# Cross attention of a two-block network: the order of its four units, where softmax reads from, and where its outputs go

## The chip, the cores and the metric

The kernel runs on one core of a Trainium2 chip. TensorE (PE in the profile) does matmuls and transposes, VectorE (DVE) and ScalarE (ACT) do elementwise work, SyncE (SP) and GpSimd (POOL) start transfers. PE writes to PSUM, eight banks of 128 partitions x 512 float32; everything else lives in SBUF. The metric is the device time of one execution in microseconds, as a median of several.

## The reference

Two blocks of layers on a sequence of 256 tokens, width 2048. The change touches only the cross attention of the second block: 256 queries against 256 memory rows, 4 heads of 128.

```python
def memory_cross_attention(hn, mem_n, w_q, w_kv, w_o):
    ...
    q = (hn @ w_q).reshape(B, S, CROSS_HEADS, CROSS_HEAD)
    k, v = split_cols_2(mem_n @ w_kv, (CROSS_HEADS * CROSS_HEAD, CROSS_HEADS * CROSS_HEAD))
    ...
    s = jnp.einsum('bshd,bmhd->bhsm', q, k).astype(jnp.float32) * (CROSS_HEAD ** -0.5)
    prob = jax.nn.softmax(s, axis=-1).astype(v.dtype)
    o = jnp.einsum('bhsm,bmhd->bshd', prob, v).reshape(B, S, CROSS_HEADS * CROSS_HEAD)
    return o @ w_o
```

Before it stands `h = h + mix(...)`, behind it the up and down products of the feed-forward part.

## The kernel before

Every engine has one instruction stream of its own, written by hand, and semaphores between them. Most of the time goes into large products that are done as `stream`s of **chunks**. A chunk is 512 rows of a weight matrix by 512 columns (1 MB). SP loads it into one of four buffers `weights_raw`; ACT copies it, rounded to float32r, into one of two buffers `weights_hi` (L671, function `hi`); DVE writes the rest, raw minus hi, into `weights_lo` (L1257, function `lo`); PE does 24 matmuls of 512 columns with it (L2054): the high part of the activations times both parts, and their low part times the high one. The activations of a product are therefore needed as two tiles, `acts_hi` and `acts_lo`. ACT may split chunk c when PE is through with chunk c-2 of the whole program (`chunk_used`), DVE follows ACT (`hi_ready`), PE follows DVE (`lo_ready`), and SP may load over a raw buffer once DVE has read it.

Four PSUM banks (0 to 3) hold the sums of the streams. The other four are a ring for everything else: each **job** in the list `job_counts` takes the next one, so a job waits until the job four places before it was read (`bank_free`), its reader waits until it is written (`bank_full`), and whoever needs the copy waits for the reader (`copied`).

The stage in question: `stream(cross_kv)` makes keys and values, `stream(cross_q)` (one block, four chunks) the queries; both come out through ACT (L687) in natural layout. PE transposes keys (`ckT`) and queries (`cqT`), two jobs each of four 128x128 transposes (L2125), ACT copies them (L951). Then come four **units** u, each a pair of heads and a half of the queries. For each unit PE computes scores (L2375, one bank of 2x256), DVE scales and copies them to SBUF (L1662), takes their row maximum (L1668) and negates it (L1669); ACT takes the exponentials in place with their row sums (L1028); DVE inverts the sums (L1675) and multiplies (L1677); PE transposes the probabilities (L2385, one bank of 4x128), ACT copies them (L1016); PE multiplies them with the values (L2396) and ACT copies the result to `acts_T` (L1022). PE's order is scores(0), scores(1), probs(0), outputs(0), scores(2), probs(1), outputs(1), scores(3), and so on; the probabilities have two buffers. When all four results are in `acts_T`, ACT and DVE split them (L786, L1327) for `stream(cross_o)`, a product with four blocks of one chunk each, whose first chunk they split only then. DVE adds each block to the residual (L2005).

Names that the text uses: `hi(0)`, `lo(0)` are the splits of the first chunk of `cross_o`; `hi(1)`, `lo(1)` those of the second.

Of the kernel before, what the change touches and what calls it, by code (L numbers as in the profile page):

```python
# [7 lines left out]
F32 = mybir.dt.float32  # L8
F32R = mybir.dt.float32r
I32 = mybir.dt.int32  # L10
ALU = mybir.AluOpType
# [4 lines left out]
P = 128  # L16
# [118 lines left out]
def build(nc, a, out, stop=None):  # L135
# [129 lines left out]
    CSP = place("cross_probs", 195.5, [P, 2, 2, T])  # L265
    CPT = place("cross_probs_T", 199.5, [P, 2, NB])
# [100 lines left out]
    def attention_jobs(pre, units):  # L367
        out_ = []
        for u in range(units + 1):
            if u < units:  # L370
                out_.append((f"{pre}_s{u}", 1))
            if u >= 1:
                out_ += [(f"{pre}_p{u - 1}", 1), (f"{pre}_o{u - 1}", 1)]
        return out_

# [12 lines left out]
    job_counts += attention_jobs("cross", 4)  # L388
# [77 lines left out]
    ACTS = {"ctx": 0, "lat": 4, "mix": 8, "cross_o": 12}  # L466
# [195 lines left out]
    def _(eng):  # L662
# [346 lines left out]
        def attention_steps(pre, SPb, PTb, dst, f0):  # L1009

            def probs_copy(u):
                jj = J[f"{pre}_p{u}"]
                if u >= 2:
                    bank_full(eng, J[f"{pre}_o{u - 2}"])
                bank_full(eng, jj)
                free(eng.activation(PTb[:, u % 2, :], bank(jj), ACT.Copy), jj)  # L1016

            def out_copy(u):
                pair, half = u // 2, u % 2
                jj = J[f"{pre}_o{u}"]  # L1020
                bank_full(eng, jj)
                free(eng.activation(dst[:, f0 + 2 * pair:f0 + 2 * pair + 2, half * P:(half + 1) * P],  # L1022
                                    bank(jj)[:, 0:T].rearrange("p (a b) -> p a b", a=2), ACT.Copy), jj)

            def exps(u):
                eng.wait_ge(S(pre + "_shifted"), u + 1)
                for e in range(2):
                    ch.add(eng.activation(SPb[:, u % 2, e, :], SPb[:, u % 2, e, :], ACT.Exp,  # L1028
                                          bias=STAT[:, 64 + 4 * (u % 2) + e:65 + 4 * (u % 2) + e],
                                          accum_out=STAT[:, 66 + 4 * (u % 2) + e:67 + 4 * (u % 2) + e]))  # L1030
                ch.done(pre + "_exp")

            return exps, probs_copy, out_copy

        def softmax_rows(pre, units, SPb, PTb, dst, f0):
            exps, probs_copy, out_copy = attention_steps(pre, SPb, PTb, dst, f0)
            for u in range(units):
                exps(u)
                if u >= 1:
                    probs_copy(u - 1)  # L1040
                    out_copy(u - 1)
            probs_copy(units - 1)
            out_copy(units - 1)

# [206 lines left out]
    def _(eng):  # L1251
# [399 lines left out]
        def attention_steps(pre, SPb, scale, bias):  # L1651

            def shift(u):
                half = u % 2
                m = 64 + 4 * (u % 2)
                if u >= 2:
                    bank_full(eng, J[f"{pre}_p{u - 2}"])
                jj = J[f"{pre}_s{u}"]
                bank_full(eng, jj)
                sc = bank(jj).rearrange("p (a b) -> p a b", a=2)  # L1660
                if bias is None:
# [21 lines left out]
        def softmax_rows(pre, units, SPb, scale, bias):  # L1683
            shift, divide = attention_steps(pre, SPb, scale, bias)
            for u in range(units):
                shift(u)
                divide(u)
# [1121 lines left out]
```

## Time and profile before

| | |
|---|---|
| median of 3 runs | 2879.57 us (2877.43 to 2879.62) |
| the profiled execution | 2869.85 us, span 2868.0 us |
| PE busy | 2574.4 us, 90% of the span |
| DVE, ACT busy | 1373.8 us (48%), 1102.1 us (38%) |
| chain that ended last | PE 59%, DVE 9%, ACT 4% |
| granted TensorE clock, mean | 0.922 of 2.4 GHz |

The span runs from the first to the last instruction that the profile shows. All times in rows are microseconds from its start. PE's matmul rows overlap each other, so its busy time is larger than its share of the chain. The granted clock is 1.00 at 2.4 GHz and 0.50 at 1.2 GHz; values between are means over a stretch in which both occurred.

### The profile page before, as it was taken

The page shows a single profiled execution, that of the slowest core. Times are in us where ns is not written, and L with a number is a line of the kernel's source. Part 1 is how long each engine was busy: PE and PEld are TensorE (multiplying, and loading weights), DVE is VectorE, ACT ScalarE, POOL GpSimd, SP SyncE. Part 2 cuts the span into 40 slices and gives each one's busy share as a digit, 9 for nine tenths or more (in the row PEclk, how much of TensorE's full clock was granted, in tenths as well). Part 3 has the DMA queues.
Part 4 walks back from the last instruction along what each step waited for, and adds up shares of the span by engine and source line. Part 5 has one row for each costly group of instructions (what it writes and reads, how often), then busy time and mean ns, then how long its engine had stood idle before and what let it go on. Part 6 is the DMA issues. An engine that isn't in the chain of part 4 may idle for free.

```text
span 2868.0 us, 30832 instructions
## 1 busy us (share of the span) xinstructions
PE 2574.4 (90%) x12600; PEld 2040.4 (71%) x12600; DVE 1373.8 (48%) x1331; ACT 1102.1 (38%) x1105; POOL 44.0 (2%) x77
## 2 busy tenths in 40 slices
PE   5799999999798999797999776889779999999996
PEld 0486787886477677576888655677668888888885
DVE  0234434557736533457444585444345544544543
ACT  1434435343333333434433343234444433434332
POOL 0000000001000000000000000000000000000000
PEclk8798989999998999798999677889889999999998
DMA  9843434558954774454554000254235555555553
GB/s 392 305 150 132 147 123 145 176 191 344 386 190 149 249 257 168 153 186 134 185 185 141 1 7 23 72 190 161 88 117 177 191 191 191 188 190 186 186 197 109
DMA packets 227546, 498.68 MB, mean 174 GB/s; under 512 B 25144, under 2 KB 27192, under 8 KB 218080
## 3 DMA queue, kind: packets, MB, share of 16 engines
q1 hardware_dynamic: 220752, 459.44, 46.8%
q0 software_dynamic: 6672, 37.51, 3.5%
q8 instruction: 90, 1.47, 0.2%
q14 instruction: 32, 0.26, 0.0%
HBM read 493.24 MB, written 3.67 MB: 173 GB/s over the span
## 4 chain that ended last, share of the span: by engine, by line
PE 59%; DVE 9%; ACT 4%; DMA 1%; issue 1%; DVEq 0%; POOL 0%; ACTq 0%
PE banks L2054 52%; DVE weights_lo L1257 1%; DMA raw_eight<-in_w_ada 1%; ACT weights_hi L671 1%; PE banks L2125 1%; ACT acts_hi L752 1%; PE banks L2512 1%; DVE index_scores L1756 1%; PE banks L2339 1%; DVE shifted_tile L1318 1%; PE banks L2260 1%; PE banks L2297 1%; PE banks L2355 0%; PE banks L2580 0%; PE banks L2243 0%
## 5 line engine op out<-in xcount | busy, mean ns | idle before, releaser
L1257 DVE TENSOR_TENSOR weights_lo<-weights_raw,weights_hi 128x2048 fp32r<-128x2048 f32 (+3 forms) x368 | 815.6, 2219 | 1042.4 <-ACT weights_hi L671 1041.5
L671 ACT ACTIVATE weights_hi<-weights_raw 128x2048 fp32r<-128x2048 f32 (+3 forms) x368 | 682.4, 1858 | 1142.0 <-PE banks L2054 1138.6
L2054 PE MATMUL banks<-weights_hi,acts_hi 128*128 128x512 f32 (+3 forms) x2432 | 967.5, 398 | 92.6 <-DVE weights_lo L1257 81.7
L2054 PE MATMUL banks<-weights_lo,acts_hi 128*128 128x512 f32 (+3 forms) x2432 | 956.0, 393 | 0.0
L2054 PE MATMUL banks<-weights_hi,acts_lo 128*128 128x512 f32 (+3 forms) x2432 | 955.4, 393 | 0.0
L2054 PEld LDWEIGHTS banks<-weights_hi,acts_hi 128*128 128x128 f32 x2432 | 476.0, 196 | 212.0 <-issue 76.3
L2054 PEld LDWEIGHTS banks<-weights_hi,acts_lo 128*128 128x128 f32 x2432 | 475.7, 196 | 94.7
L2054 PEld LDWEIGHTS banks<-weights_lo,acts_hi 128*128 128x128 f32 x2432 | 476.9, 196 | 92.1 <-issue 1.0
L2054 PE MATMUL banks<-weights_hi,hidden_hi 128*128 128x512 f32 x256 | 99.9, 390 | 0.0
L2054 PE MATMUL banks<-weights_hi,hidden_hi_odd 128*128 128x512 f32 x256 | 99.8, 390 | 0.0
L2054 PE MATMUL banks<-weights_hi,hidden_lo 128*128 128x512 f32 x256 | 99.7, 389 | 0.0
L2054 PE MATMUL banks<-weights_hi,hidden_lo_odd 128*128 128x512 f32 x256 | 99.7, 389 | 0.0
L2054 PE MATMUL banks<-weights_lo,hidden_hi 128*128 128x512 f32 x256 | 99.7, 389 | 0.0
L2054 PE MATMUL banks<-weights_lo,hidden_hi_odd 128*128 128x512 f32 x256 | 99.7, 389 | 0.0
L2147 PE MATMUL banks<-raw_eight,cond 128*2 128x512 f32 x256 | 54.6, 946 | 46.6 <-DMA raw_eight<-in_w_ada 36.6
L2147 PEld LDWEIGHTS banks<-raw_eight,cond 128*2 128x2 f32 x256 | 3.6, 83 | 94.0 <-DMA raw_eight<-in_w_ada 83.1
L2054 PEld LDWEIGHTS banks<-weights_hi,hidden_lo 128*128 128x128 f32 x256 | 48.1, 188 | 10.1
L2054 PEld LDWEIGHTS banks<-weights_hi,hidden_hi_odd 128*128 128x128 f32 x256 | 48.1, 188 | 10.0
L2054 PEld LDWEIGHTS banks<-weights_hi,hidden_lo_odd 128*128 128x128 f32 x256 | 48.1, 188 | 10.0
L2054 PEld LDWEIGHTS banks<-weights_lo,hidden_hi_odd 128*128 128x128 f32 x256 | 48.1, 188 | 9.9
L2054 PEld LDWEIGHTS banks<-weights_lo,hidden_hi 128*128 128x128 f32 x256 | 48.1, 188 | 9.9
L2054 PEld LDWEIGHTS banks<-weights_hi,hidden_hi 128*128 128x128 f32 x256 | 48.1, 188 | 9.9
(481 smaller groups left out, 1943.0 us busy)
## 6 DMA issues: line engine op xcount, KB each, us to landing
raw_eight<-in_w_ada SPq DMA_DIRECT2D x80, 1024.0 KB, 17.0
weights_raw<-in_w_in_e SPq DMA_DIRECT2D x80, 1024.0 KB, 5.3
weights_raw<-in_w_up SPq DMA_DIRECT2D x64, 1024.0 KB, 5.4
weights_raw<-in_w_down SPq DMA_DIRECT2D x64, 1024.0 KB, 5.0
weights_raw<-in_w_in SPq DMA_DIRECT2D x44, 1024.0 KB, 5.1
weights_raw<-in_w_in_o SPq DMA_DIRECT2D x32, 1024.0 KB, 5.3
weights_raw<-in_w_out_e SPq DMA_DIRECT2D x16, 1024.0 KB, 5.5
gate_chunks<-in_w_ada POOLq DMA_DIRECT2D x16, 1024.0 KB, 5.8
```

The lines of the kernel that those rows point to most:

```text
L671: eng.activation(WHI[:, c % 2, :, 0:n], RAW[:, sl, :, 0:n], ACT.Copy).then_inc(hi_ready, 1)
L752: ins = eng.activation(xh[:, f0 + f, :], bank(jj)[:, e * T:(e + 1) * T], func or ACT.Identity, scale=scale(f), bias=bias(f) if bias else 0.0)
L1257: eng.tensor_tensor(WLO[:, c % 2, :, 0:n], RAW[:, c % 4, :, 0:n], WHI[:, c % 2, :, 0:n].bitcast(F32), ALU.subtract).then_inc(lo_ready, 1)
L1318: ch.link(eng.tensor_scalar(TILE[:, e, :], src, scale(f), bias(f), ALU.mult, ALU.add))
L1756: ch.link(eng.scalar_tensor_tensor(out=SC[:, half, :], in0=RL[:, j % 2, e, :], scalar=KIWI[:, half, 64 + hd:65 + hd], in1=SC[:, half, :], ...
L2054: ins = eng.matmul(BANKS[:, par * 2 + h, 0:s.n], x[:, t, h * P:(h + 1) * P], w[:, c % 2, k, 0:s.n], start=(kc == 0 and k == 0 and m == 0), ...
L2125: ins = eng.transpose(bank(jj)[:, (f % 2) * T + h * P:(f % 2) * T + (h + 1) * P], src(f, h), ident)
L2147: ins = eng.matmul(BANKS[32 * j:32 * j + 2, 2 * hf, :], CF[:, kt, :], RAW8[:, m % 8, j, :], start=(kt == 0), stop=(kt == KT - 1))
L2260: ins = eng.matmul(bank(jj)[:, o0:o0 + P], A[:, 2 * hd + k2, h * P:(h + 1) * P], B[:, 2 * hd + k2, h * P:(h + 1) * P], start=(k2 == 0), st ...
L2297: ins = eng.matmul(dst, DECAYED[16 + d][:, 2 * hd + k2, B * P:(B + 1) * P], S0[:, d, hd, k2, :], start=False, stop=(d == 1 and k2 == 1))
L2339: ins = eng.matmul(bank(jj)[32 * j:32 * j + 2, :], CF[:, m, :], GCH[:, m % 2, j, :], start=(m == 0), stop=(m == KT - 1))
L2512: ins = eng.matmul(bank(jj)[:, q * P:(q + 1) * P], A[r, f, half * P:(half + 1) * P], B[r, f, half * P:(half + 1) * P], start=True, stop=True)
```

## The change

Six edits, all in this stage:

1. The transposes of the keys move from behind `stream(cross_q)` to behind its second chunk on PE, and their copies on ACT from behind it to the place after the sum of squares that follows its last split.
2. All four scores come first on PE, each in a ring bank of its own; then probs(0), probs(1), probs(2), outputs(0), probs(3), outputs(1), outputs(2), outputs(3). The ring's order follows. `cross_probs` gets four buffers, `cross_probs_T` keeps two.
3. DVE's scaled copy is gone. The maximum is read from PSUM, the exponential too, with the scale inside the activation.
4. The statistics have a place for each unit, so no unit waits for another's.
5. `acts_T` is left out: ACT copies each unit's output from PSUM to `acts_hi`, DVE subtracts that from PSUM into `acts_lo`.
6. The attention steps of ACT and DVE now stand inside `stream(cross_o)`, behind the split of its first chunk: `hi(0)` and `lo(0)` come before the first exponential and the first maximum.

```diff
+    job_counts += [(f"cross_s{u}", 1) for u in range(4)]
+    job_counts += [(f"cross_{n}", 1) for n in ("p0", "p1", "p2", "o0", "p3", "o1", "o2", "o3")]
...
-        stream(st["cross_q"], after={3: lambda: rms_squares(XN, 4, Y)})
-        tiles_out("ckT", CKT)
+        stream(st["cross_q"], after={3: lambda: (rms_squares(XN, 4, Y), tiles_out("ckT", CKT))})
         tiles_out("cqT", CQT)
-        softmax_rows("cross", 4, CSP, CPT, XS, 0)
-        wait_jobs("cross_o3")
-        split_hi(XS, 0)
-        stream(st["cross_o"])
+
+        def cross_exp(u):
+            eng.wait_ge(S("cross_max"), u + 1)
+            jj = J[f"cross_s{u}"]
+            for e in range(2):
+                ins = eng.activation(CSP[:, u, e, :], bank(jj)[:, e * T:(e + 1) * T], ACT.Exp, scale=128.0 ** -0.5,
+                                     bias=STAT[:, 64 + 4 * u + e:65 + 4 * u + e],
+                                     accum_out=STAT[:, 66 + 4 * u + e:67 + 4 * u + e])
+                if e == 0:
+                    ch.add(ins)
+            free(ins, jj)
+            copied(eng, jj)
+            ch.done("cross_exp")
+
+        def cross_probs_copy(u):
+            if u >= 2:
+                bank_full(eng, J[f"cross_o{u - 2}"])
...
+        def cross_hi(u):
+            jj = J[f"cross_o{u}"]
+            bank_full(eng, jj)
+            ch.add(eng.activation(cross_tiles(XTH, u), bank(jj)[:, 0:T].rearrange("p (a b) -> p a b", a=2), ACT.Copy))
+            ch.done("cross_hi")
+
+        def cross_attention():
+            for step, u in ((cross_exp, 0), (cross_exp, 1), (cross_exp, 2), (cross_probs_copy, 0), (cross_exp, 3),
+                            (cross_probs_copy, 1), (cross_probs_copy, 2), (cross_hi, 0), (cross_probs_copy, 3),
+                            (cross_hi, 1), (cross_hi, 2), (cross_hi, 3)):
+                step(u)
+
+        stream(st["cross_o"], after={0: cross_attention})
...
-        softmax_rows("cross", 4, CSP, 128.0 ** -0.5, None)
-        split_lo(XS, (0,), ACTS["cross_o"])
-        stream(st["cross_o"], sum_block(st["cross_o"], "h_block"))
+
+        def cross_max(u):
+            m = 64 + 4 * u
+            jj = J[f"cross_s{u}"]
+            bank_full(eng, jj)
+            ch.link(eng.tensor_reduce(STAT[:, m:m + 2], bank(jj).rearrange("p (a b) -> p a b", a=2), AX.X, ALU.max))
+            ch.add(eng.tensor_scalar(STAT[:, m:m + 2], STAT[:, m:m + 2], -(128.0 ** -0.5), None, ALU.mult))
+            ch.done("cross_max")
...
+        def cross_lo(u):
+            pair, half = u // 2, u % 2
+            jj = J[f"cross_o{u}"]
+            eng.wait_ge(S("cross_hi"), u + 1)
+            bank_full(eng, jj)
+            xl, xh = [t[:, 2 * pair:2 * pair + 2, half * P:(half + 1) * P] for t in (XTL, XTH)]
+            free(eng.tensor_tensor(xl, bank(jj)[:, 0:T].rearrange("p (a b) -> p a b", a=2), xh.bitcast(F32),
+                                   ALU.subtract), jj)
+
+        def cross_attention():
+            for step, u in ((cross_max, 0), (cross_max, 1), (cross_divide, 0), (cross_max, 2), (cross_divide, 1),
+                            (cross_max, 3), (cross_divide, 2), (cross_divide, 3), (cross_lo, 0), (cross_lo, 1),
+                            (cross_lo, 2), (cross_lo, 3)):
+                step(u)
+
+        stream(st["cross_o"], sum_block(st["cross_o"], "h_block"), after={0: cross_attention})
...
+        def cross_keys():
+            eng.wait_ge(block_out, 4 + 2 * st["cross_q"].b0)
+            transposes("ckT", natural(CKV))
+
+        stream(st["cross_q"], after={1: cross_keys})
         eng.wait_ge(block_out, 4 + 2 * st["cross_o"].b0)
-        transposes("ckT", natural(CKV))
         transposes("cqT", natural(CQ))
         jobs_out(eng, "cqT")
-        attention("cross", 4, CQT, CKT, lambda hd: hd, lambda g, sh: CKV[:, 1, sh, g * P:(g + 1) * P], CSP, CPT)
...
+        for u in range(4):
+            cross_scores(u)
+        for step, u in ((cross_probs, 0), (cross_probs, 1), (cross_probs, 2), (cross_outputs, 0), (cross_probs, 3),
+                        (cross_outputs, 1), (cross_outputs, 2), (cross_outputs, 3)):
+            step(u)
         stream(st["cross_o"])
```

What stands on PE from the first scores on, before. The rows with `cross_k_T` are scores, those with `constants` are transposes of the probabilities, those with `cross_probs_T` are outputs; a `side_free` is the release of a ring bank.

```order
L2375 MATMUL banks<-cross_k_T,cross_q_T 128x256 [waits side_free3,side_free2,side_free1,side_free0]
L2375 MATMUL banks<-cross_k_T,cross_q_T 128x256
L2375 MATMUL banks<-cross_k_T,cross_q_T 128x256 [waits side_free3]
L2375 MATMUL banks<-cross_k_T,cross_q_T 128x256
L2385 MATMUL banks<-constants,cross_probs 128x128 [waits side_free0,cross_probs]
L2385 MATMUL banks<-constants,cross_probs 128x128 x3
L2396 MATMUL banks<-cross_probs_T,cross_kv 128x128 [waits side_free1,side_free0]
L2396 MATMUL banks<-cross_probs_T,cross_kv 128x128 x3
L2375 MATMUL banks<-cross_k_T,cross_q_T 128x256 [waits side_free2]
L2375 MATMUL banks<-cross_k_T,cross_q_T 128x256
```

The same place on PE in the changed kernel, from the third unit's scores on.

```order
L2699 MATMUL banks<-cross_k_T,cross_q_T 128x256 [waits side_free0]
L2699 MATMUL banks<-cross_k_T,cross_q_T 128x256
L2699 MATMUL banks<-cross_k_T,cross_q_T 128x256 [waits side_free1]
L2699 MATMUL banks<-cross_k_T,cross_q_T 128x256
L2709 MATMUL banks<-constants,cross_probs 128x128 [waits side_free2,cross_probs]
L2709 MATMUL banks<-constants,cross_probs 128x128 x3
L2709 MATMUL banks<-constants,cross_probs 128x128 [waits side_free3,cross_probs]
L2709 MATMUL banks<-constants,cross_probs 128x128 x3
L2709 MATMUL banks<-constants,cross_probs 128x128 [waits side_free0,cross_probs]
L2709 MATMUL banks<-constants,cross_probs 128x128 x3
L2720 MATMUL banks<-cross_probs_T,cross_kv 128x128 [waits side_free1,side_free2]
L2720 MATMUL banks<-cross_probs_T,cross_kv 128x128 x3
```

Scores of units 2 and 3 no longer stand behind the outputs of units 0 and 1, and three transposes stand ahead of the first output.

DVE in the changed kernel, from the last step before the attention on (L1326 belongs to `stream(cross_q)`).

```order
L1326 RECIPROCAL inverse_rms<-inverse_rms 128x2 [waits dve_steps,root_out]
L1246 TENSOR_TENSOR weights_lo<-weights_raw,weights_hi 128x2048 [waits dve_steps,hi_ready]
L1974 TENSOR_REDUCE stats<-banks 128x2 [waits side_full2]
L1975 TENSOR_SCALAR stats<-stats 128x2 [waits dve_steps]
L1974 TENSOR_REDUCE stats<-banks 128x2 [waits dve_steps,side_full3]
L1975 TENSOR_SCALAR stats<-stats 128x2 [waits dve_steps]
L1981 RECIPROCAL stats<-stats 128x2 [waits dve_steps,cross_exp]
L1983 TENSOR_SCALAR cross_probs<-cross_probs,stats 128x256 [waits dve_steps]
L1983 TENSOR_SCALAR cross_probs<-cross_probs,stats 128x256
L1974 TENSOR_REDUCE stats<-banks 128x2 [waits dve_steps,side_full0]
```

The first row that reads scores (L1974) stands behind a whole `weights_lo` of 2048 columns, which before came after the attention.

ACT in the changed kernel, from the copies of the queries on.

```order
L943 ACTIVATE cross_q_T<-banks 128x512 [waits side_full0]
L943 ACTIVATE cross_q_T<-banks 128x512 [waits side_full1]
L663 ACTIVATE weights_hi<-weights_raw 128x2048 [waits chunk_used,chunk_landed0]
L1194 ACT_TABLE_LOAD
L1194 ACTIVATE cross_probs,stats<-banks,stats 128x256 [waits cross_max]
L1194 ACTIVATE cross_probs,stats<-banks,stats 128x256
```

`weights_hi` of the first chunk moved from behind the attention to the place before the table load and the first exponential.

## Rows read from the trace of the kernel before

**Rows 1.** The chain that ended last, 2040 to 2115 us: start, length, what.

```profile
2056.42 1.27 ACT cross_q L687 x2
...
2061.74 0.70 DVE cross_probs L1662
...
2063.44 1.10 ACT cross_probs L1028 x4
...
2088.03 0.39 ACT acts_T L1022
...
2088.50 1.06 ACT acts_hi L786
...
2089.73 1.92 ACT weights_hi L671
...
2091.67 2.30 DVE weights_lo L1257
...
2094.11 20.96 PE banks L2054 x83
```

**Rows 2.** Timeline of PE: start, length, group, idle time before it and what ended it.

```profile
2057.74 1.09 PE L2125 MATMUL banks<-constants,cross_kv 128*128 128x128 f32 x8 [1.42 <-ACT cross_q L687]
2058.67 1.04 PE L2125 MATMUL banks<-constants,cross_q 128*128 128x128 f32 x8
2060.60 1.97 PE L2375 MATMUL banks<-cross_k_T,cross_q_T 128*128 128x256 f32 x8 [0.89 <-ACT cross_q_T L951]
2065.54 0.66 PE L2385 MATMUL banks<-constants,cross_probs 128*128 128x128 f32 x4 [2.98 <-DVEq L451]
2069.14 2.07 PE L2396 MATMUL banks<-cross_probs_T,cross_kv 128*128 128x128 f32 x8 [2.95 <-ACT cross_probs_T L1016]
...
2072.72 1.06 PE L2385 MATMUL banks<-constants,cross_probs 128*128 128x128 f32 x4
2076.61 1.21 PE L2396 MATMUL banks<-cross_probs_T,cross_kv 128*128 128x128 f32 x8 [2.83 <-ACT cross_probs_T L1016]
```

**Rows 3.** Timeline of ACT, same columns.

```profile
2060.51 1.28 ACT L1028 ACT_TABLE_LOAD   x1
...
2068.50 0.60 ACT L1016 ACTIVATE cross_probs_T<-banks 128x512 f32<-128x512 f32 x1
...
2101.79 1.92 ACT L671 ACTIVATE weights_hi<-weights_raw 128x2048 fp32r<-128x2048 f32 x1 [8.35 <-PE banks L2054]
2107.23 1.92 ACT L671 ACTIVATE weights_hi<-weights_raw 128x2048 fp32r<-128x2048 f32 x1 [3.52 <-PE banks L2054]
```

**Rows 4.** Timeline of DVE, same columns.

```profile
2063.18 0.17 DVE L1669 TENSOR_SCALAR stats<-stats 128x2 f32<-128x2 f32 x1
2064.61 0.17 DVE L1675 RECIPROCAL stats<-stats 128x2 f32<-128x2 f32 x1 [1.26 <-ACTq L451]
2064.81 0.62 DVE L1677 TENSOR_SCALAR cross_probs<-cross_probs,stats 128x256 f32<-128x256 f32 x2
```

**Rows 5.** Groups by line and shape: busy us, mean ns, idle before.

```profile
L1886 DVE TENSOR_REDUCE stats<-banks 128x2 f32<-128x512 f32 x4 | 2.8, 692 | 11.7 <-PE banks L2557 11.6
...
L1886 DVE TENSOR_REDUCE stats<-banks 128x2 f32<-128x256 f32 x4 | 1.7, 424 | 7.1 <-PE banks L2557 7.1
...
L1135 ACT ACTIVATE probs<-banks,stats 128x256 f32<-128x256 f32 x8 | 3.7, 469 | 19.7 <-DVEq L451 19.7
```

**Rows 6.** Windows from start to end: length, busy PE, PEld, DVE, ACT, POOL, granted clock, DMA.

```profile
2066.00:2074.00 8.00, 4.83 (x18) 3.77 (x16) 2.83 (x8) 2.07 (x6) 0.00 (x0) 0.58 0.00 0
2074.00:2078.00 4.00, 1.39 (x9) 1.35 (x10) 1.40 (x5) 1.83 (x6) 0.00 (x0) 0.93 0.00 0
...
2085.00:2098.00 13.00, 6.14 (x18) 4.92 (x18) 5.72 (x3) 5.75 (x5) 0.00 (x0) 0.50 0.21 64
2098.00:2104.00 6.00, 6.00 (x27) 4.88 (x26) 1.55 (x3) 1.92 (x1) 0.00 (x0) 0.99 0.60 213
```

**Rows 7.** DMA issues of SP: start, length, op, count.

```profile
2032.08 18.09 SPq L499 DMA_DIRECT2D weights_raw<-in_w_o_cross  x4
```

More of the change, by code:

```diff
@@ L463, in acc @@
         return BANKS[:, (B % 2) * 2 + h, :]
[L466 removed]
+    ACTS = {"ctx": 0, "lat": 4, "mix": 8}
     def mlp_streams(stream, tile_step, at, first=None):
@@ L1007, in _ @@
         rms_squares.n = 0
[L1009 to L1043, printed above, removed]
         eng.wait_ge(S("norm_cols"), 2)
@@ L2744, in _, with cross_scores, cross_probs, cross_outputs @@
         transposes("x3T", natural(XN), ("h_block", 0))
-        stream(st["cross_q"])
+        def cross_keys():
+            eng.wait_ge(block_out, 4 + 2 * st["cross_q"].b0)
+            transposes("ckT", natural(CKV))
+        stream(st["cross_q"], after={1: cross_keys})
         eng.wait_ge(block_out, 4 + 2 * st["cross_o"].b0)
-        transposes("ckT", natural(CKV))
         transposes("cqT", natural(CQ))
         jobs_out(eng, "cqT")
-        attention("cross", 4, CQT, CKT, lambda hd: hd, lambda g, sh: CKV[:, 1, sh, g * P:(g + 1) * P], CSP, CPT)
+        def cross_scores(u):
+            pair, half = u // 2, u % 2
+            jj = J[f"cross_s{u}"]
+            bank_free(eng, jj)
+            for e in range(2):
+                ins = eng.matmul(bank(jj)[:, e * T:(e + 1) * T], CQT[:, 2 * pair + e, half * P:(half + 1) * P],
+                                 CKT[:, 2 * pair + e, :], start=True, stop=True)
+            full(ins, jj)
+        def cross_probs(u):
+            eng.wait_ge(S("cross_probs"), u + 1)
+            jj = J[f"cross_p{u}"]
+            bank_free(eng, jj)
+            for e in range(2):
+                for sh in range(2):
+                    ins = eng.transpose(bank(jj)[:, (2 * e + sh) * P:(2 * e + sh + 1) * P],
+                                        CSP[:, u, e, sh * P:(sh + 1) * P], ident)
+            full(ins, jj)
+        def cross_outputs(u):
+            copied(eng, J[f"cross_p{u}"])
+            jj = J[f"cross_o{u}"]
+            bank_free(eng, jj)
+            for e in range(2):
+                g = 2 * (u // 2) + e
+                for sh in range(2):
+                    ins = eng.matmul(bank(jj)[:, e * P:(e + 1) * P], CKV[:, 1, sh, g * P:(g + 1) * P],
+                                     CPT[:, u % 2, (2 * e + sh) * P:(2 * e + sh + 1) * P], start=(sh == 0),
+                                     stop=(sh == 1))
+            full(ins, jj)
+        for u in range(4):
+            cross_scores(u)
+        for step, u in ((cross_probs, 0), (cross_probs, 1), (cross_probs, 2), (cross_outputs, 0), (cross_probs, 3),
+                        (cross_outputs, 1), (cross_outputs, 2), (cross_outputs, 3)):
+            step(u)
         stream(st["cross_o"])
```

100 lines of the change are left out of this document (17 added, 83 removed).

## The prediction

> **What bounds the kernel now.** I read the page first: PE is busy for 90% of the span, and the chain that ended last is PE for 59%. Almost everywhere an engine that gets faster gains nothing. So the question is whether the attention is one of the places where PE waits. I read the chain in order of time there: it goes from the last matmul of `stream(cross_q)` (2056.4 us) to the first of `stream(cross_o)` (2094.11) through ACT, PE and DVE in turn, never through two at once [rows 1]. These 37.7 us contain four times the same round of scores, copy and maximum, exponential, division, transposes, copy, outputs. Then come two serial splits, of `acts_T` (1.06 us and more) and of the first chunk of weights (1.92 + 2.30). PE's timeline shows the waits between, 2.8 to 3.0 us each before probabilities and outputs [rows 2]. No transfer is part of this. Last I read the granted clock: it is 0.58 over 2066 to 2074, 0.93 over 2074 to 2078, 0.50 over 2085 to 2098 and 0.99 behind that [rows 6]. It fell after PE had mostly idled and rose after it had worked with few gaps. So PE's work here has two prices: four transposes 0.66 or 1.06, one unit's outputs 1.21 or 2.07 [rows 2].
>
> **The change, as a schedule on the clock of the trace before.**
>
> *Keys ahead (edit 1).* Eight transposes take 0.93 us on PE (2058.67 - 2057.74) [rows 2]. PE is the bound inside `stream(cross_q)`, so its end moves by +0.93. ACT's two key copies come out of the tail, where the query copies stood behind them: about -1.0 (two copies of 0.60 less their overlap) [rows 3]. They now lie in ACT's idle time before 2056.4, between its last split and the query's evacuation. Sum: nothing, -0.1. The query copies end at 2060.44 where they ended at 2060.51.
>
> *First chunk ahead (edit 6).* ACT does `hi(0)`, 1.92, to 2062.4, then the table load, 1.28 [rows 3], to 2063.7. DVE waits for `hi(0)`, does `lo(0)`, 2.30 [rows 1], to 2064.75, and only then the first maximum; behind it queue all DVE steps of the attention, and ACT waits for the maximum. Before, DVE began at 2061.74. This costs 3.0 us at the head. The four scores (twice 1.97 for two units [rows 2]) run from 2060.5 to 2064.2 under it and are free. The table load is covered too: without the cover it would cost 1.28. The load of this chunk was issued at 2032 [rows 7], nearly 30 us earlier, so nobody waits for it.
>
> *Softmax (edits 2 to 4).* The scaled copy, 0.70 per unit, is gone [rows 1]. The maximum from PSUM costs 0.69, the exponential of 256 from PSUM 0.47, as other attention in this kernel shows [rows 5]; a pair with its sums I take as before, 1.10 [rows 1]. So maximum plus negation with gaps: 0.69 + 0.17 + 0.04 = 0.90; inversion plus multiplications: 0.17 + 0.03 + 0.62 = 0.82, 0.86 with gaps [rows 4]. DVE is the slower of the two. Its order gives: maximum 0 to 2065.7, exponential 0 to 2066.85, maximum 1 beside it, division 0 to 2067.75, maximum 2 to 2068.7, division 1 to 2069.6, maximum 3 to 2070.5, division 2 to 2071.4, exponential 3 to 2071.6, division 3 to 2072.5. PE transposes each unit behind its division; its third set goes from 2071.45 to 2072.1 or 2072.5, by the clock. The copy of unit 0 (0.60) stands on ACT behind exponential 2 and is ready at 2070.45, that of unit 1 at 2072.25.
>
> *Outputs (edits 2 and 5).* From here PE's own order is the chain: outputs 0, transposes 3, outputs 1, 2, 3. The bank of outputs 0 was that of scores 3, free at 2071.6, which is early enough. Copy 2 waits for outputs 0 and copy 3 for outputs 1, since there are two buffers; either is ready 0.65 behind, while PE has other work for at least that long. At 1.2 GHz: 2.07 + 0.95 + three times 1.9 = 8.7, to 2081.2. At 2.4 GHz: 1.2 + 0.6 + three times 1.1 = 5.1, to 2077.2. Then `hi` of the last unit, 0.38 by the copy in [rows 1], and its low part: 128x256 from PSUM is not in the trace in this form; 424 ns by the reduction of the same shape at one end [rows 5], 0.69 by a full bank at the other. I take 0.42, nearest in shape. With hops 0.95 together. PE starts `cross_o` at 2082.2 or 2078.1, where it started at 2094.11: 11.9 or 16.0 us gained.
>
> *Second chunk.* `hi(1)` and `lo(1)` now start when the attention ends and take 1.92 + 2.30 + 0.1 = 4.3. PE is in chunk 0 for 7.68 us (2094.11 to 2101.79), or 5.44 at the high clock (2101.79 to 2107.23) [rows 1, 3]. So they are hidden; without that cover they would take back 4.3. With `lo(0)` early SP may issue one load of the next weights about 29 us sooner, into an idle queue: nothing.
>
> *Chunk 0 and the clock.* Its 7.68 contains 2.2 us at the low clock. If the dense stretch before it already brought the high one, these are saved as well.
>
> **Sum.** Low clock to the end: 11.9. High clock throughout: 16.0 + 2.2 = 18.2. The unknown is when the clock comes back. Before, it came back at 2098, 4 us after PE had started on dense work; and about 2074, again with PE dense since 2069 [rows 2, 6]. In the changed kernel PE is dense from 2071.45 on, about 10 us. So I take the return near 2076, between the ends: it shortens the last outputs by about 2, and probably keeps half of the 2.2. That is 11.9 + 2 + 1.1 = 15.0 us. Against the profiled execution (2869.85) that is 2854.9. The median of the runs shown is 9.7 above it; I subtract the same 15.0 from the median: 2864.6.
>
> **Rivals.**
> *The clock stays low through the attention and all of chunk 0.* PE's gaps around 2062 to 2071 grow with `lo(0)` in front, which speaks for a fall; the long dense stretch behind speaks against its lasting. 24 matmuls at 0.43 would be 10.2 us instead of 7.68, so the gain is 11.9 - 2.6 = 9.3: 2870.3.
> *The clock returns early,* before outputs 1. Then nearly everything of the 18.2 is gained, less outputs 0: about 17.3, 2862.3. The Trainium skill says so too (TensorE: Matmul & The Clock Gate, Part 1): low is the default, and sustained matmul activity releases it. The restart at 2094 to 2098 agrees with this.
> *The gain is given back behind the stage.* `stream(cross_o)` might then wait for its later chunks or the feed-forward part for weights. Each split of the later chunks follows a chunk of PE by 4.2 us of work under 5.44 of cover, only 1.2 of slack [rows 3]. If DVE's residual sums got in between, three chunks could lose a few us each; 10 us or more would leave 2877 or no change. Against it: the order there is the same as before.
> *Slower: the split at the head becomes the wait.* ACT and DVE stand in order behind `hi(0)`. If its raw chunk or its buffer came late, all four units would wait, one for one. It starts to cost more than the change gains when it is 15 us late, and shows as slower at 21 us: 2886 or more. The issue time of the load [rows 7] and the chunk two places ahead, which PE finished near 2051 (one chunk of 5.44 before 2056.4), speak against it by 10 us and more.
>
> **Chances.** Forecast with a return of the clock inside the stage, early or in the middle: 0.76, range 2861 to 2868. Low clock: 0.14, 2868 to 2872. Given back: 0.07. Slower: 0.03. A measurement of this kernel tells about 0.2%, 5.8 us, from no change. So faster 0.90, same 0.07, slower 0.03. The range reaches from the high clock throughout (2861.4, and 1.5 for the scatter of medians, 2.2 us between the runs shown) to the low clock (2870.3 and 1): 2860 to 2871.
>
> **What would show it.** Right: no row of a scaled copy; `weights_lo` of 2.3 us ending just before the first maximum, about 2064.8; all scores done before it; the first matmul of `cross_o` at 2078 to 2082, 12 to 16 us earlier; behind it no wait of PE for the second chunk; the copies of keys before the last evacuation. Each step is wrong where its group is elsewhere: a wait of PE inside the outputs for a copy would mean that the two buffers bind; a wait of the first exponential for the table load that its cover fails; one at the second chunk that the split there isn't hidden. The prediction fails most easily by the granted clock between 2068 and 2086, and by anything outside the stage, since 15 us are only 0.5% of the whole.

## The result, and the profile after

Six executions of the changed kernel have a median of 2857.2 us (2850.7 to 2858.8), six of the kernel before, the three of the table above among them, 2877.48 us (2867.26 to 2879.62). The ratio is 0.9937, with a 95% interval of 0.992 to 0.9954: clearly faster, by 13 to 23 us. The forecast of 2864.6 had the direction right. Its range, 2860 to 2871, did not hold the time. The profiled executions took 2853.41 us (changed) and 2869.85 us (before; this one is not among the six).

First the page of the changed kernel: span, busy time, chain.

```profile
span 2851.6 us, 30842 instructions
...
PE 2566.1 (90%) x12600; PEld 2033.9 (71%) x12600; DVE 1371.6 (48%) x1330; ACT 1100.1 (39%) x1104; POOL 44.0 (2%) x77
...
PE 60%; DVE 9%; ACT 4%; DMA 1%; issue 1%; DVEq 0%; POOL 0%; ACTq 0%
```

It looks as before. A stage of 30 us is 1% of the span, so the page cannot show what happened in it. The chain can; from the copies of the queries to chunk 0 of `cross_o`:

```profile
2059.06 1.81 ACT weights_hi L663
2060.89 2.29 DVE weights_lo L1246
2063.18 0.61 DVE stats L1974
...
2064.08 1.03 ACT cross_probs L1194 x4
...
2065.40 0.63 DVE cross_probs L1983 x2
...
2066.16 0.70 DVE stats L1974
...
2069.41 0.63 DVE cross_probs L1983 x2
...
2070.14 1.11 PE banks L2709 x4
2071.25 1.71 PE banks L2720 x8
2072.96 0.85 PE banks L2709 x4
2073.81 3.70 PE banks L2720 x24
2077.53 0.39 ACT acts_hi L1217
...
2078.00 0.44 DVE acts_lo L1992
2078.43 0.41 issue
2078.84 6.17 PE banks L2035 x26
```

Read it against [rows 1]. The split of the first chunk stands at the head (2059.06 to 2063.18). Then DVE is the chain to 2070.04, with the exponentials of the first unit once between, one unit in 2.0 us; and then PE alone for 7.4 us. What was four rounds through three engines is now one stretch of DVE and one of PE. `cross_o` starts at 2078.84, where it started at 2094.11.

PE's timeline around it, first the key transposes inside `stream(cross_q)`, then scores and first transposes, and two rows of ACT's: the key copies, and the split that waits for the end of chunk 0.

```profile
2043.97 1.03 PE L2109 MATMUL banks<-constants,cross_kv 128*128 128x128 f32 x8
2044.76 0.47 PE L2035 MATMUL banks<-weights_hi,acts_hi 128*128 128x512 f32 x1
...
2059.16 3.69 PE L2699 MATMUL banks<-cross_k_T,cross_q_T 128*128 128x256 f32 x16 [0.79 <-ACT cross_q_T L943]
2066.13 1.11 PE L2709 MATMUL banks<-constants,cross_probs 128*128 128x128 f32 x4 [3.27 <-DVEq L443]
...
2051.00 1.09 ACT L943 ACTIVATE cross_k_T<-banks 128x512 f32<-128x512 f32 x2 [0.33 <-DVEq L1636]
2055.97 1.26 ACT L679 ACTIVATE cross_q<-banks,inverse_rms 128x512 f32<-128x512 f32 x2 [3.88 <-PE banks L2035]
...
2084.67 1.92 ACT L663 ACTIVATE weights_hi<-weights_raw 128x2048 fp32r<-128x2048 f32 x1 [4.66 <-PE banks L2035]
```

Windows: length, busy PE, PEld, DVE, ACT, POOL, granted clock, DMA share, GB/s. The clock is low from 2066 to 2075.8 and high from there on. Before it rose PE had worked without a wait since the third set of transposes at 2070.14, for 5.7 us. Compare [rows 6], where it was low over the last 13 us as well.

```profile
2066.00:2071.00 5.00, 3.09 (x12) 2.30 (x13) 3.99 (x14) 3.50 (x12) 0.00 (x0) 0.50 0.35 134
2071.00:2075.80 4.80, 4.80 (x25) 4.80 (x24) 0.52 (x2) 1.12 (x3) 0.00 (x0) 0.50 0.00 0
2075.80:2078.00 2.20, 1.70 (x15) 1.51 (x14) 0.85 (x3) 1.39 (x4) 0.00 (x0) 1.00 0.00 0
```

**A measure free of the rest.** The executions of one kernel lie up to 18 us apart (the kernel before, 2863.8 to 2881.6), far more than the terms in question. I therefore compare two times inside each profile: **gap**, from the start of ACT's evacuation of the queries to PE's first matmul of `cross_o`, and **chunk 0**, from there to the start of ACT's third split of `cross_o`, which waits for that chunk (the second in the timeline of the changed kernel after the attention). Before: 2094.11 - 2056.42 = 37.69 and 2101.79 - 2094.11 = 7.68, together 45.37 [rows 1, 3]. Changed: 2078.84 - 2055.97 = 22.87 and 2084.67 - 2078.84 = 5.83, together 28.70. From the end of chunk 0 to the end of the span all fourteen profiles of this study agree within 1.4 us (765.8 to 767.2).

These 1.4 us arise at one place. Up to 26.9 us behind chunk 0 all profiles run alike; then PE starts the first feed-forward product after a wait of 5.15 us, in all of them at the low clock. How long it stays low differs, the rise comes 30 to 33 us behind chunk 0: in the kernel before at 2132.2 (30.4 behind), in the changed kernel at 2116.8 (32.1 behind). The rows are windows of the two kernels from that start on.

```profile
2128.73:2132.10 3.37, 3.37 (x8) 2.69 (x9) 2.05 (x1) 0.00 (x0) 0.00 (x0) 0.50 0.66 184
2132.30:2134.00 1.70, 1.70 (x9) 1.40 (x8) 0.00 (x0) 0.00 (x0) 0.00 (x0) 1.00 1.06 370
...
2111.59:2116.70 5.11, 5.11 (x12) 4.05 (x13) 2.06 (x1) 0.00 (x0) 0.00 (x0) 0.50 0.76 251
2116.90:2119.00 2.10, 2.10 (x11) 1.73 (x10) 0.00 (x0) 0.00 (x0) 0.00 (x0) 1.00 0.83 307
```

So a difference of 1 or 2 us in the sum can shrink or grow by up to 1.4 us by the end of the kernel.

### The profile page after: what moved, and what is told of

The parts are those of the page before. It is cut to its first block, busy times and chain, and to the rows that moved or that the text cites. A ratio compares the mean times of both kernels' runs of the same rounds, so it can differ in the third digit from the quotient of the medians.

```text
span 2851.6 us, 30842 instructions
## 1 busy us (share of the span) xinstructions
PE 2566.1 (90%) x12600; PEld 2033.9 (71%) x12600; DVE 1371.6 (48%) x1330; ACT 1100.1 (39%) x1104; POOL 44.0 (2%) x77
## 4 chain that ended last, share of the span: by engine, by line
PE 60%; DVE 9%; ACT 4%; DMA 1%; issue 1%; DVEq 0%; POOL 0%; ACTq 0%
PE banks L2035 52%; DVE weights_lo L1246 1%; DMA raw_eight<-in_w_ada 1%; ACT weights_hi L663 1%; PE banks L2109 1%; PE banks L2451 1%; ACT acts_hi L744 1%; DVE index_scores L1707 1%; PE banks L2323 1%; DVE shifted_tile L1307 1%; PE banks L2244 1%; PE banks L2281 1%; PE banks L2339 0%; PE banks L2519 0%; PE banks L2227 0%
## 6 DMA issues: line engine op xcount, KB each, us to landing
raw_eight<-in_w_ada SPq DMA_DIRECT2D x80, 1024.0 KB, 16.7
```

## The experiments

All are edits of the changed kernel unless said otherwise. "Sum" is gap plus chunk 0, from one profile each; medians stand beside the kernel before as it was timed with them.

| kernel | gap | chunk 0 | sum | median us (runs) | before, timed with it |
|---|---|---|---|---|---|
| before | 37.69 | 7.68 | 45.37 | 2877.48 (6) | |
| before_again | 38.95 | 8.47 | 47.42 | 2875.72 (12) | 2873.22 (17) |
| before_gap | 38.78 | 5.81 | 44.59 | 2868.88 (10) | 2869.71 (13) |
| changed | 22.87 | 5.83 | 28.70 | 2857.20 (6) | 2877.48 (6) |
| after_again | 22.71 | 5.80 | 28.51 | 2857.11 (5) | 2870.36 (14) |
| keys_behind | 23.64 | 5.83 | 29.47 | 2859.37 (4) | 2874.87 (9) |
| sequential | 30.37 | 7.42 | 37.79 | 2862.41 (10) | 2870.36 (14) |
| copy_kept | 24.27 | 5.81 | 30.08 | 2858.89 (4) | 2873.22 (17) |
| via_acts | 23.16 | 7.42 | 30.58 | 2856.43 (4) | 2874.87 (9) |
| split_behind | 23.51 | 7.33 | 30.84 | 2857.81 (5) | 2870.36 (14) |
| split_early | 20.56 | 5.83 | 26.39 | 2853.22 (5) | 2870.36 (14) |
| filler | 20.07 | 5.82 | 25.89 | 2854.31 (4) | 2874.87 (9) |
| best | 19.05 | 5.79 | 24.84 | 2853.00 (5) | 2874.87 (9) |
| best_filler | 15.93 | 5.81 | 21.74 | 2850.51 (5) | 2873.22 (17) |

**after_again and before_again: both kernels once more.** No edit. Expected of the first, and of the second:

> The changed kernel once more, timed side by side with the one before. In the two profiles the stage accounts for 16.3 us (14.8 from the evacuation of the queries to the first matmul of cross_o, 1.9 in the first chunk, 0.4 given back by the key transposes), while the medians differ by 20.3. Theory A (the schedule of the prediction holds, the rest is scatter of single executions): 14.5 to 18.5 us faster. Theory B (something outside the stage, such as the granted clock of later stages, adds to it): 19 to 22 us faster, and the profiles differ by more than the stage.

> The kernel before, unchanged, timed against itself. It was profiled once, and its medians were 2877.5, 2870.4 and 2874.9 us on three occasions. Scatter theory: single executions differ by up to 12 us outside the stage (the nine profiles have their first 862 us between 860.8 and 867.0, and the next 1195 between 1191.4 and 1198.3), while from the evacuation of the queries to the end it takes 811.6 within 1 us as in its first profile; the two medians agree within 5 us. Rival (the stage itself scatters by its clock, so that the 16 us of the two profiles are luck): 809 or less, or 814 or more, from the evacuation to the end.

The changed kernel: ratio 0.9952 (0.9938 to 0.9966), 13.3 us between the medians instead of 20.3, below both expectations (14.5 to 18.5, and 19 to 22). The changed kernel itself had the same median both times, 2857.2 and 2857.11; what moved was the kernel before, from 2877.48 to 2870.36. The stage took the same, 28.51 against 28.70. The kernel before against itself: 1.0009 (0.9997 to 1.002), medians 2.5 us apart. But its stage took 47.42, not 45.37. PE and ACT in its second profile (compare 1.21 for a set of outputs in [rows 2] and the 7.68):

```profile
2080.09 1.64 PE L2396 MATMUL banks<-cross_probs_T,cross_kv 128*128 128x128 f32 x8 [2.83 <-ACT cross_probs_T L1016]
...
2098.85 0.77 PE L2054 MATMUL banks<-weights_hi,acts_hi 128*128 128x512 f32 x1 [6.11 <-DVE weights_lo L1257]
...
2107.32 1.92 ACT L671 ACTIVATE weights_hi<-weights_raw 128x2048 fp32r<-128x2048 f32 x1 [9.14 <-PE banks L2054]
```

The waits of PE are nearly those of the first profile (2.83 and 6.11 us in both); PE's work is longer, since the clock changed at other moments. So the stage before is worth 45.4 to 47.4 us, and the gain of the change in it 16.7 to 18.9. Counted from the evacuation to the end of the span it is 16.0 to 18.3 (811.6 and 813.9 less 795.6). From the evacuation to the end this profile took 813.9, at the border between the two expectations: the scatter theory was too narrow, the rival's "luck" is real, but 2 us and not more.

**sequential: the old order of units (edit 2 undone).**

```diff
-        for u in range(4):
-            cross_scores(u)
-        for step, u in ((cross_probs, 0), (cross_probs, 1), (cross_probs, 2), (cross_outputs, 0), (cross_probs, 3),
-                        (cross_outputs, 1), (cross_outputs, 2), (cross_outputs, 3)):
+        for step, u in ((cross_scores, 0), (cross_scores, 1), (cross_probs, 0), (cross_outputs, 0), (cross_scores, 2),
+                        (cross_probs, 1), (cross_outputs, 1), (cross_scores, 3), (cross_probs, 2), (cross_outputs, 2),
+                        (cross_probs, 3), (cross_outputs, 3)):
```

The ring of banks and the steps of ACT and DVE follow the same order.

> The changed kernel with the units in the order of the kernel before (scores of units 2 and 3 behind the outputs of 0 and 1, ring of banks accordingly), all other edits kept. Theory A: keys, scaled copies, direct outputs and split are worth 37.7 - 1.0 - 2.8 - 4.7 + 3.0 = 32.2 us from evacuation to cross_o, so the order alone is worth 9.3; 9 to 11 us slower than the changed kernel. Rival (the shorter chain of each unit is the main thing, the order hides little since DVE is the bound): 3 to 5 us slower.

37.79: 9.1 us above the changed kernel; from the evacuation to the end 8.5, the medians timed together 5.3 apart. Theory A said 9 to 11, the rival 3 to 5. The profile bears out the theory, the medians lie between the two. PE waits for each unit's probabilities again, and then 1.18 us before `cross_o`:

```profile
2076.52 1.42 PE L2719 MATMUL banks<-cross_probs_T,cross_kv 128*128 128x128 f32 x8 [2.25 <-ACT cross_probs_T L1207]
...
2082.54 1.16 PE L2719 MATMUL banks<-cross_probs_T,cross_kv 128*128 128x128 f32 x8 [2.04 <-ACT cross_probs_T L1207]
...
2087.28 0.56 PE L2034 MATMUL banks<-weights_hi,acts_hi 128*128 128x512 f32 x1 [1.18 <-DVE acts_lo L1991]
```

7.5 us of the 9.1 are the gap (30.37, where I had worked out 32.2), 1.6 are chunk 0, partly at the low clock (0.50 from 2087.8 to 2090.9). The order is about half of the 16.7 to 18.9 us in the profiles, and 5.3 of 13.3 in the medians.

**copy_kept: the scaled copy on DVE again (edit 3 undone).**

```diff
-            ch.link(eng.tensor_reduce(STAT[:, m:m + 2], bank(jj).rearrange("p (a b) -> p a b", a=2), AX.X, ALU.max))
...
+            free(eng.tensor_scalar(CSP[:, u], bank(jj).rearrange("p (a b) -> p a b", a=2), 128.0 ** -0.5, None,
+                                   ALU.mult), jj)
+            copied(eng, jj)
+            ch.link(eng.tensor_reduce(STAT[:, m:m + 2], CSP[:, u], AX.X, ALU.max))
...
```

ACT takes the exponentials in place in SBUF again.

> The changed kernel with edit 3 undone: DVE copies the scaled scores to SBUF first and takes the maximum there, ACT works in place. Theory A (DVE is the bound of the softmax part): 0.72 per unit on DVE, three to four of them on the path before the third set of transposes: 2.2 to 2.9 us more, 797.8 to 798.5 from the evacuation to the end (795.6 in the changed kernel). Rival (PE's outputs at the low clock are the bound, so a later softmax meets a higher clock and loses half of it): 796.5 to 797.

The third set of transposes starts 17.04 us after the evacuation (2076.55 - 2059.51) where the changed kernel has 14.17 (2070.14 - 2055.97): the 2.9 us of theory A. But at `cross_o` only 1.4 to 1.6 are left (a gap of 24.27 against 22.87 and 22.71):

```profile
2073.83 1.11 PE L2707 MATMUL banks<-constants,cross_probs 128*128 128x128 f32 x4 [1.61 <-DVEq L443]
2076.55 1.12 PE L2707 MATMUL banks<-constants,cross_probs 128*128 128x128 f32 x4 [1.61 <-DVEq L443]
...
2079.17 0.69 PE L2707 MATMUL banks<-constants,cross_probs 128*128 128x128 f32 x4
2079.70 2.90 PE L2718 MATMUL banks<-cross_probs_T,cross_kv 128*128 128x128 f32 x24
```

The last three sets of outputs took 2.90 instead of 3.90. PE came to them later, with the clock up from the start. DVE is the bound of the softmax, as theory A says, and the rival is right that a later PE gets half back: 796.3 us from the evacuation to the end, in neither range, but nearer to the rival's.

**via_acts: outputs through `acts_T` (edit 5 undone).**

```diff
-            ch.add(eng.activation(cross_tiles(XTH, u), bank(jj)[:, 0:T].rearrange("p (a b) -> p a b", a=2), ACT.Copy))
-            ch.done("cross_hi")
+            free(eng.activation(cross_tiles(XS, u), bank(jj)[:, 0:T].rearrange("p (a b) -> p a b", a=2), ACT.Copy), jj)
...
+            wait_jobs("cross_o3")
+            split_hi(XS, 0)
```

> The changed kernel with edit 5 undone: outputs go to acts_T and are split there when all are in. Theory A: behind the last output 0.38 + 1.06 + 1.23 and gaps instead of 0.38 + 0.42, so 1.9 us later to cross_o (24.7 instead of 22.8 from the evacuation), and chunk 0 up to 1.9 us longer if PE's gap of 3.2 us brings the clock down: 797.5 to 799.4 from the evacuation to the end. Rival (the four direct low parts on DVE and their semaphores cost as much as they save): within 0.5 us of the changed kernel.

PE's wait before `cross_o` is 2.96 instead of 1.35, and chunk 0 takes 7.42 (2086.94 - 2079.52) instead of 5.83, as expected:

```profile
2073.66 2.90 PE L2718 MATMUL banks<-cross_probs_T,cross_kv 128*128 128x128 f32 x24
...
2079.52 0.47 PE L2036 MATMUL banks<-weights_hi,acts_hi 128*128 128x512 f32 x1 [2.96 <-issue]
...
2086.94 1.92 ACT L663 ACTIVATE weights_hi<-weights_raw 128x2048 fp32r<-128x2048 f32 x1 [6.74 <-PE banks L2036]
```

The sum is only 1.9 above, and `cross_o` starts only 0.3 later instead of 1.9, because in this execution the last three outputs met the high clock (2.90). The median, 2856.43, is no slower than the changed kernel's 2857.2 and 2857.11, which were timed at other times; 2 us are below what 4 runs tell. From the evacuation to the end it is 796.7, between theory A's range and the rival's.

**split_behind and split_early: where the first chunk is split (edit 6).** The first undoes the edit, the second moves both splits into the time in which PE works on the last chunk of `cross_q`, where ACT and DVE are idle. `stream(cross_o)` then leaves out the split of its first chunk (this part is not shown).

```diff
-        stream(st["cross_o"], after={0: cross_attention})
+        cross_attention()
+        stream(st["cross_o"])
```

```diff
+        stream(st["cross_q"], after={3: lambda: (rms_squares(XN, 4, Y), tiles_out("ckT", CKT),
+                                                      hi(st["cross_o"], st["cross_o"].g0, 0, 0))})
...
+        stream(st["cross_q"], after={3: lambda: (inverse_rms(4), lo(st["cross_o"], st["cross_o"].g0, 0, 0))})
```

> The changed kernel with edit 6 undone: the first chunk of cross_o is split behind the attention. Theory A: the head is 2.8 us shorter (the first maximum follows the scores at once), the tail 3.5 longer (1.92 + 2.29 less what the last low part hides), and PE's longer gap makes chunk 0 up to 2 us longer by its clock. From evacuation to cross_o 23.6 us instead of 22.9; 0.7 to 2.8 us slower than the changed kernel. Rival (the split ahead is the main gain, as its 4.3 us suggest): 4 us or more slower.

> The changed kernel with hi(0) and lo(0) moved further ahead, to the idle time of ACT and DVE before the last chunk of cross_q ends. Theory A (the split stands on the path at the head): the first maximum starts 2.8 us earlier, from evacuation to cross_o 20.1 us, 2.8 us faster than the changed kernel. Rival 1 (the granted clock sets the end of the attention): PE's gaps shrink, the clock does not fall, and the gain is 4 to 6 us. Rival 2 (the head is hidden by something else, as the table load): 1 us or less.

Behind: the head is shorter, the wait before `cross_o` 4.98 us instead of 1.35, and chunk 0 takes 7.33, the clock 0.50 in it up to 2086.1. The sum is 2.1 to 2.3 us more, 0.6 to 0.8 of it in the gap and 1.5 in chunk 0; from the evacuation to the end 1.0 is left, and the medians are 0.7 apart. All this is inside theory A's 0.7 to 2.8; the rival's 4 us are not there. Early:

```profile
2061.61 5.38 PE L2702 MATMUL banks<-cross_k_T,cross_q_T 128*128 128x256 f32 x16 [0.79 <-ACT cross_q_T L944]
2067.27 0.66 PE L2712 MATMUL banks<-constants,cross_probs 128*128 128x128 f32 x4 [0.28 <-DVEq L443]
...
2056.40 2.29 DVE L1248 TENSOR_TENSOR weights_lo<-weights_raw,weights_hi 128x2048 fp32r<-128x2048 f32 x1 [3.01 <-ACT weights_hi L663]
2063.63 0.69 DVE L1977 TENSOR_REDUCE stats<-banks 128x2 f32<-128x512 f32 x1 [4.93 <-PE banks L2702]
```

The low part is done at 2058.7 in DVE's idle time, and the first maximum comes 5.21 us after the evacuation instead of 7.13. 2.1 to 2.3 us are gained in the sum, 3.9 between the medians timed together. The scores fell into a low clock here (5.38 instead of 3.69), and DVE waits 0.78 for the second of them; that this cost as much of the gain is an argument and was not tried.

**keys_behind: the keys behind `cross_q` again (edit 1 undone).** `tiles_out("ckT", CKT)` and `cross_keys()` stand where they stood.

> The changed kernel with edit 1 undone: the key transposes and copies stand behind stream(cross_q) again. Measured inside the profile, from the evacuation of the queries to the end, the changed kernel took 795.6 us. Theory A: 0.8 us less PE work inside cross_q (the changed kernel's eight transposes there take 2043.97 to 2044.76) and 1.0 us more behind it: 796.6 there, and the whole within 0.3 us of the changed kernel. Rival (moving them is worth the whole key work, about 2 us, since PE had room inside cross_q): 797.5 and 1.5 to 2 us slower in all.

The sum is 0.8 to 1.0 us more, and the 0.79 us of PE work inside `cross_q` (2044.76 - 2043.97) are saved: nothing, as expected.

**filler: the clock by itself.**

```diff
+        def busy(n):
+            for _ in range(n):
+                eng.matmul(BANKS[:, 2, :], XTH[:, 8, 0:P], WHI[:, 1, 0, :], start=True, stop=True)
...
+        busy(12)
+        for step, u in ((cross_probs, 0), (busy, 3), (cross_probs, 1), (busy, 3), (cross_probs, 2),
...
```

> The changed kernel with 18 extra matmuls of 512 columns on PE into an unused sum bank: 12 behind the scores, 3 behind each of the first two sets of transposes. They compute nothing that is used. Clock theory: the granted clock does not fall at 2066, the outputs run at 1.2 us each from the first, and cross_o starts 2 to 2.5 us earlier in spite of the extra work; 793.1 to 793.6 from the evacuation to the end. Rival (the clock was not what lengthened the outputs, or the extra matmuls hold up the transposes that stand behind them): the same as the changed kernel or up to 1 us slower.

```profile
2072.16 1.06 PE L2720 MATMUL banks<-cross_probs_T,cross_kv 128*128 128x128 f32 x8
2073.05 0.60 PE L2709 MATMUL banks<-constants,cross_probs 128*128 128x128 f32 x4
2073.49 2.90 PE L2720 MATMUL banks<-cross_probs_T,cross_kv 128*128 128x128 f32 x24
...
2056.00:2084.00 28.00, 22.87 (x125) 18.61 (x124) 13.37 (x27) 15.74 (x32) 0.00 (x0) 1.00 0.17 51
```

The outputs take 1.06 + 0.60 + 2.90 instead of 1.91 + 1.06 + 3.90, the clock is 1.00 throughout (the last row is the window from 2056 to 2084), and the sum is 2.6 to 2.8 us smaller, although PE does 18 matmuls more. In the profiles the clock is a term of its own. The median, 2854.31 of 4 runs, was not timed beside the changed kernel.

**before_gap: the clock of chunk 0 in the kernel before.** 12 such matmuls behind the last outputs of the kernel before.

> The kernel before with 12 extra matmuls of 512 columns on PE between the last outputs and cross_o, where PE waits 6.1 us for the two splits; nothing uses their result. Clock theory: chunk 0 took 7.7 and 8.5 us in the two profiles of the kernel before because PE came to it from a gap; with the gap filled the clock is up at its start or soon behind it, chunk 0 takes 5.5 to 6.2, and from the evacuation of the queries to the end it is 809.5 to 812 (811.6 and 813.9 in the two profiles). So some 2 us of the change's gain is clock alone and could be had without any reordering. Rival (at 1.2 GHz the extra matmuls outlast the gap, or the clock does not return in time): no gain or 0.5 us slower.

```profile
2088.40 3.98 PE L2752 MATMUL banks<-acts_hi 128*128 128x512 f32 x12
...
2094.86 0.47 PE L2054 MATMUL banks<-weights_hi,acts_hi 128*128 128x512 f32 x1 [2.48 <-DVE weights_lo L1257]
...
2100.67 1.92 ACT L671 ACTIVATE weights_hi<-weights_raw 128x2048 fp32r<-128x2048 f32 x1 [6.48 <-PE banks L2054]
```

Chunk 0 takes 5.81 instead of 7.68 and 8.47. The gap is 38.78, no shorter than before, since two of the outputs in it met the low clock (1.59 and 1.77 us where the first profile had 1.21 and 1.16); from the evacuation to the end it is 810.9, inside the clock theory's range. The ratio of the timed runs, 0.9997 (0.9984 to 1.0009), cannot resolve these 2 us of 2870.

**best and best_filler: the experiments put together.** The first is split_early, and PE waits for the second pair's outputs only in the middle of chunk 0. The second adds 6 matmuls, 3 behind each of the first two sets of transposes.

```diff
             for k in range(4):
                 t = kt + k
+                if k == 2 and s.acts == "cross_o" and g == s.g0:
+                    for u in (2, 3):
+                        copied(eng, J[f"cross_o{u}"])
...
             elif s.acts == "cross_o":
-                for u in range(4):
+                for u in range(2):
                     copied(eng, J[f"cross_o{u}"])
```

> split_early (20.6 us from the evacuation to cross_o, 793.0 to the end), and PE waits before chunk 0 only for the outputs of the first pair of heads, and for the second pair's in the middle of the chunk. Theory A: the wait of 1.34 us before cross_o lies under half a chunk (12 matmuls, 2.7 us): cross_o starts 1.3 us earlier, 791.7 from the evacuation to the end, 4 us faster than the changed kernel. Rival (the last outputs, not the wait behind them, end the stage, so that the wait only moves into the chunk): 793.0.

> The version called best with 6 extra matmuls of 512 columns, 3 behind each of the first two sets of transposes, to keep PE's clock up there. Clock theory: outputs take 1.06 + 0.6 + 2.9 us instead of 1.77 + 1.06 + 3.45, so 1.7 us less: 790.3 from the evacuation to the end, where best has 792.0. Rival (without the 12 matmuls behind the scores the clock falls anyway): 792 to 792.5.

best: 1.5 us less than split_early, all of it in the gap, as theory A said; ratio to before 0.9921 (0.9907 to 0.9936). best_filler: 21.74, 3.1 less again, of which 1.7 were expected and the other 1.4 lie ahead of the first transposes, by the clock of the scores in that execution (3.69 against 5.38); ratio 0.9919 (0.9906 to 0.9932). The two intervals overlap, so the added matmuls are worth nothing that these runs can tell. In the medians best lies 4 us below the changed kernel, but the two were not timed together.

## Why the prediction was wrong

The gap was forecast well. I had the evacuation at 2057.35 and `cross_o` at about 2080.2, a gap of 22.85: measured 22.87 and 22.71. That it fits to the tenth is in part luck, since terms below were off by 0.2 to 0.4 us and made up for each other.

- *Keys ahead: nothing.* Shown by keys_behind: 0.8 to 1.0 more behind, 0.79 less inside.
- *First chunk ahead: 3.0 at the head, hidden behind.* The first maximum came 7.13 us after the evacuation, I had 7.4. The second chunk's splits were hidden, the table load too. Undoing the edit costs 2.1 to 2.3 us in the sum, splitting earlier still gains as much.
- *DVE is the bound of the softmax.* The chain shows it, and copy_kept delayed the third set of transposes by 2.9. On the path this was worth only 1.4 to 1.6, because the outputs that came later met the high clock.
- *Outputs: PE's order is the chain, the two buffers do not bind.* PE had no wait from 2070.14 to 2077.5. I had the clock's return near 2076, 4.6 us behind the start of the third transposes; it came at 2075.8, 5.7 behind it, since everything from the evacuation on came 1.4 us earlier than in my schedule. The two agree in the place, among the last outputs, and not in the time. The outputs with the transposes among them took 6.5 us, where the forecast comes to 6.7 (8.7 less 2), and the way behind them to `cross_o` 1.35 and 1.18, where I had 0.95.
- *Chunk 0.* I kept half of the 2.2 us, 1.1. In every profile of the changed kernel it took 5.80 to 5.83, so 1.85 to 2.67 us were gained. This term was too small by 0.8 to 1.6. Some 0.6 to 0.7 of it is lost again 26.9 us behind chunk 0, where the clock returned later than in the kernel before.
- *The stage before as a fixed 45.4.* Its second profile took 47.4. Its clock scatters, and the profile that I subtracted from was the shorter one. Against the two, the gain in the stage is 16.7 and 18.9, less 0.8 inside `cross_q`: about 16 and 18 us, where the forecast said 15.0. Counted to the end of the span, 15.2 and 17.5 are left.
- *The level: the step that failed.* "I subtract the same 15.0 from the median", 2879.57 of three runs, with 2.2 us for "the scatter of medians". The 71 executions of the kernel before that were timed by the end have a median of 2872.9 and go from 2863.8 to 2881.6; the three shown lay at the upper end of it, and the profiled execution, 9.7 below their median, was a sign of that. From 2872.9 the same 15.0 would have given 2857.9, and 2854.9 from the profiled execution, where the changed kernel's took 2853.41. So 6.7 of the miss of 7.4 us are the level from which I subtracted; 0.7 is left for the size of the gain. The eleven executions of the changed kernel have a median of 2857.1, 15.8 below 2872.9, which is within the 15.2 to 17.5 of the profiles. By the same reading, 20.3 us between the two medians of six is more than the change is worth, and 13.3 less than the profiles say.

The rival of an early return of the clock gave 17.3 us, between the two gains in the stage. Its mechanism is wrong in the place: the clock returned during the last outputs and not before outputs 1. What it had right is chunk 0. That rival came to 2862.3, so it missed the time by the same level. The rivals of a gain given back and of a late split did not occur: the time behind chunk 0 is the same in all profiles within 1.4 us, and that much is the clock at the next restart.

What stays open: why the executions of one kernel differ by up to 18 us. The evacuation of the queries starts between 2055.97 and 2063.18 us in the fourteen profiles, and all but edit 1 and the early split lie behind it. So nearly all of this scatter of 7 us belongs to code that no edit touches (edit 1 adds 0.8). Which waits make it was not tried.

## What to carry to other kernels

Where several small engines pass one unit of work around, put all units' first steps ahead in each engine's stream, and let each engine do its share in one run; this order was worth 9 us of 17 to 19 in the profiles here and 5 of 13 in the medians, more than dropping the copy, the direct outputs or the early split, each about 2 us or less. Price PE's work after a gap at both clock levels, and the work behind it too: waits cost a second time there (chunk 0 took 5.8 us at the high clock and 7.3 to 8.5 where a part of it ran at the low one). Where PE must wait anyway, matmuls that nobody uses shortened the stage by 2.6 to 2.8 us in one profile and by about 1.7 in another; the timed runs could not confirm it. Before subtracting a gain from a median of three runs, look how far the profiled execution lies from it: that distance is a sign of how uncertain the level is.

## What the runs showed of the hardware

- Reading from PSUM costs ACT and DVE nothing here: the maximum of 128x512 takes 0.69 us from PSUM in the changed kernel and 0.69 from SBUF in copy_kept (at 2067.37 there); a unit's exponentials take 1.03 from PSUM (2064.08 in the chain above) and took 1.10 in place in SBUF [rows 1].
- The granted clock came back at 2075.8 in the changed kernel, when PE had worked without a wait since 2070.14. The Trainium skill (TensorE: Matmul & The Clock Gate, Part 1) has it that the low clock is the default and activity releases it; the trace agrees. But with the same code the four scores took 3.69 us in one execution and 5.38 in another (changed and via_acts, alike up to there), so where the clock falls cannot be read off one profile.
- PE started `cross_o` 0.41 us after the end of the last `acts_lo` in the first profile of the changed kernel, where it had to pass waits for four outputs, the weights and the sums. In the second profile it was 0.24, in the chain of after_again below. Before it was 0.14 us: 2094.11 less the end of `weights_lo` at 2091.67 + 2.30 [rows 1]. Which of the waits costs this, and why it varies, was not tried.

```profile
2082.05 0.43 DVE acts_lo L1992
2082.48 0.24 issue
```
